# Up-projections of a latent attention group: plain float32 products against three float32r products of split operands

## The reference, cut to what matters

```
proj = h @ w_in                                   # all projections of both groups
q_a, ckv, krope, g_a, q_b, k_b, v_b, ... = split(proj)
ckv = rmsnorm(ckv, kv_gain)                       # 512 latent columns per row
q_lat = einsum('bthn,hnc->bthc', q_a[..., :128], w_uk)
s = einsum('bthc,bsc->bhts', q_lat, ckv) + einsum('bthr,bsr->bhts', q_rope, krope)
p = softmax(where(chunk_mask, s * 192 ** -0.5, -inf))
o_lat = einsum('bhts,bsc->bthc', p, ckv)
o_a = einsum('bthc,hvc->bthv', o_lat, w_uv)       # 8 heads of 128
```

## Time and profile before

| | |
|---|---|
| time, median of 3 runs | 908.91 us |
| span of the profiled execution | 907.6 us |
| PE busy | 883.5 us, 97% |
| DVE busy | 414.4 us, 46% |
| ACT busy | 322.4 us, 36% |
| DMA read from HBM, written | 175.93 MB, 12.69 MB |
| share of L1926 (`kn`) and L1935 (`vm`) in the chain that ended last | 2% each |

### The profile page before, as it was taken

How to read it: one execution, slowest core, us unless ns; L and a number is a source line. 1 busy time by engine, 2 the same in 40 slices (tenths; PEclk the granted TensorE clock), 3 DMA queues, 4 the chain that set the end, 5 groups by cost and what they waited for, 6 DMA issues and landing times.

```text
span 907.6 us, 13732 instructions
## 1 busy us (share of the span) xinstructions
PE 883.5 (97%) x5564; PEld 769.2 (85%) x5564; DVE 414.4 (46%) x851; ACT 322.4 (36%) x599; POOL 117.3 (13%) x187
## 2 busy tenths in 40 slices
PE   4999999999999999999999999999999999999996
PEld 1567688999998688888999989999999998888886
DVE  3523343336322145443333368364455566677362
ACT  3232352434321234222322264232334345554252
POOL 0000012101100000112120401000122223530000
PEclk9999999999999999999999999999999999999998
DMA  9999957464443122557552476655798833793313
GB/s 362 409 409 408 409 204 248 155 244 157 143 139 105 69 75 88 175 161 238 167 168 91 123 285 235 243 186 186 257 305 283 269 133 111 282 295 124 135 59 127
DMA packets 53439, 187.43 MB, mean 207 GB/s; under 512 B 7776, under 2 KB 8408, under 8 KB 52224
## 3 DMA queue, kind: packets, MB, share of 16 engines
q1 hardware_dynamic: 39456, 141.35, 43.0%
q0 software_dynamic: 13776, 44.68, 15.3%
q10 hardware_dynamic: 144, 0.52, 0.1%
HBM read 175.93 MB, written 12.69 MB: 208 GB/s over the span
## 4 chain that ended last, share of the span: by engine, by line
PE 89%; DMA 5%; DVE 3%; ACT 2%; issue 1%; SPq 0%; ACTq 0%; DVEq 0%
PE proj L1824 34%; PE proj L1813 29%; DMA araw<-in_units 5%; PE bankO L1794 3%; PE proj L1845 2%; PE proj L1794 2%; PE bankO L1926 2%; PE bankO L1935 2%; PE bankS L1845 1%; PE bankS L1989 1%; PE bankS L1824 1%; PE bankO L2008 1%; PE bankO L2016 1%; PE bankO L2007 1%; PE bankO L1976 1%
## 5 line engine op out<-in xcount | busy, mean ns | idle before, releaser
L1305 DVE TENSOR_TENSOR w_lo<-raw,w_hi 128x1024 fp32r<-128x1024 f32 (+2 forms) x164 | 196.9, 1205 | 236.7 <-ACT w_hi L986 235.9
L986 ACT ACTIVATE w_hi<-raw 128x1024 fp32r<-128x1024 f32 (+2 forms) x164 | 167.8, 1026 | 196.9 <-PE proj L1813 99.3
L1824 PE MATMUL proj<-hT_hi,w_hi 128*128 128x384 f32 x608 | 211.0, 347 | 0.0
L1824 PE MATMUL proj<-hT_hi,w_lo 128*128 128x384 f32 x608 | 203.8, 335 | 0.0
L1824 PE MATMUL proj<-hT_lo,w_hi 128*128 128x384 f32 x608 | 203.4, 335 | 0.0
L1813 PE MATMUL proj<-w_hi,hT_hi 128*128 128x512 f32 (+2 forms) x464 | 177.9, 384 | 0.5 <-DVE hT_lo L1564 0.4
L1813 PE MATMUL proj<-w_hi,hT_lo 128*128 128x512 f32 (+2 forms) x464 | 173.6, 374 | 0.0
L1813 PE MATMUL proj<-w_lo,hT_hi 128*128 128x512 f32 (+2 forms) x464 | 173.4, 374 | 0.0
L1824 PEld LDWEIGHTS proj<-hT_hi,w_hi 128*128 128x128 f32 x608 | 114.2, 188 | 9.5 <-issue 7.8
L1824 PEld LDWEIGHTS proj<-hT_lo,w_hi 128*128 128x128 f32 x608 | 114.3, 188 | 0.5 <-issue 0.2
L1824 PEld LDWEIGHTS proj<-hT_hi,w_lo 128*128 128x128 f32 x608 | 114.1, 188 | 0.0
(11 more groups left out here) (363 smaller groups left out, 1050.8 us busy)
## 6 DMA issues: line engine op xcount, KB each, us to landing
raw<-in_units SPq DMA_DIRECT2D x184, 512.0 KB, 4.1
araw<-in_units SPq DMA_DIRECT2D x64, 512.0 KB, 10.6
kcT<-in_dsa_k_t POOLq DMA_DIRECT2D x8, 512.0 KB, 6.4
vc<-in_cache_dsa_v POOLq DMA_DIRECT2D x8, 512.0 KB, 5.7
gate_scratch<-stage POOLq DMA_DIRECT2D x8, 384.0 KB, 3.8
raw<-in_units SPq DMA_DIRECT2D x8, 336.0 KB, 3.9
raw<-in_units SPq DMA_DIRECT2D x8, 320.0 KB, 4.9
x_sb<-in_x_prompt SPq DMA_DIRECT2D x2, 1024.0 KB, 6.1
```

The costliest lines, as they stand in the source:

```text
L986: return nc.scalar.activation(out, in_, func, scale=scale, **kw)
L1305: V.tensor_tensor(w_lo[:, SLOT[u], 0:w], raw_of(u)[:, 0:w], high(u)[:, 0:w].bitcast(F32), ALU.subtract).then_inc(lo_ready, 1)
L1824: ins = mm(banks[blk][:, 0:TOK], w[:, n, cols], a[:, kt, :], start=first and n == m == 0, stop=final and n == per - 1 and m == 2)
```

## The change

Every operand of the prompt's up-projections gets a high and a low half in float32r, and each plain float32 matmul becomes three float32r matmuls.

- `ckT` 0 and 1: ACT copies the bank as `ckv_hi`, DVE subtracts it from the bank for `ckv_lo`. The sample rows (`ckT` 2) stay plain.
- New step `uks` h, on the unit of `kn` h: ACT makes `wuk_hi` (128 x 512) of the head's `wukT`, DVE writes `wuk_lo` over `wukT`. `kn` h on PE now waits for DVE's half.
- New step `uvs` 0 to 3, on units 99, 101, 103 and 111: the same for a quarter of `wuvT` (128 x 1024 each). `wuv_lo` overwrites `wuvT`.
- Since `wuvT` is overwritten, POOL loads it a second time after `vm` for `oa` (four DMAs of 512 KB); `ld_krc`, which waits for the last `mp`, moves behind these. The first loading is listed earlier (units 87, 89, 91, 93).

```diff
@@ plan()
     for n in range(CB):
-        put(u + 15 + 4 * n, ("ld_uvT", n))
+        put(u + 13 + 2 * n, ("ld_uvT", n))
...
         if h:
-            put(u + h, ("kn", h - 1))
+            put(u + h, ("uks", h - 1), ("kn", h - 1))
+    for n, v in enumerate((LAST_UNIT["m1", 0] - 4, LAST_UNIT["m1", 0] - 2, LAST_UNIT["m1", 0], u + 2)):
+        put(v, ("uvs", n))
...
-    put(u, ("ld_krc", 0))
+    for n in range(CB):
+        put(u + 1 + n, ("ld_uvT", CB + n))
+    put(u + HEADS, ("ld_krc", 0))
@@ buffers
-    ckvT = at("ckvT", 37, [P, CB, TOK])
+    ckv_hi, ckvT = at("ckv_hi", 37, [P, CB, SEQ], F32R), at("ckvT", 41, [P, CB, P])
+    ckv_lo = at("ckv_lo", 70, [P, CB, SEQ], F32R)
+    wuv_hi = [at(f"wuv_hi{q}", kib, [P, HEADS * HD], F32R) for q, kib in enumerate((82, 86, 90, 62))]
+    wuv_lo = at("wuv_lo", 0, [P, CB, HEADS * HD], F32R)
+    wuk_hi = [at(f"wuk_hi{n}", kib, [P, CB, HD], F32R) for n, kib in enumerate((74, 95.5))]
+    wuk_lo = at("wuk_lo", 66, [P, 2, CB, HD], F32R)
@@ POOL
         def ld_uvT(q):
-            pool.wait_ge(unit_used, LAST_UNIT["ada", 3] + 1)
-            load(wuvT[:, q, :], i["w_uv_t"][:, q, :], "wuvT_in")
+            if q < CB:
+                pool.wait_ge(unit_used, LAST_UNIT["ada", 3] + 1)
+            else:
+                filled(pool, "vm", 3)
+            load(wuvT[:, q % CB, :], i["w_uv_t"][:, q % CB, :], "wuvT_in")
@@ ACT
         def ckT(t):
             filled(act, "ckT", t, "T")
+            if t < 2:
+                copy(ckv_hi[:, :, P * t:P * (t + 1)], turned).then_inc(sem("ckv_hi_ready"), 1)
+            else:
+                copy(ckvT[:], turned).then_inc(free["T"], 1)
+        def uks(h_):
+            act.wait_ge(sem(f"wukT_in{h_ % 2}"), 16 * (h_ // 2 + 1))
+            if h_ >= 2:
+                filled(act, "kn", h_ - 2)
+            copy(wuk_hi[h_ % 2][:], wukT[:, h_ % 2]).then_inc(sem("wuk_hi_ready"), 1)
+        def uvs(q):
+            if q == 0:
+                act.wait_ge(sem("wuvT_in"), 16 * CB)
+                act.wait_ge(sem("ckvn_ready"), NT)
...
+            copy(wuv_hi[q][:], wuvT[:, q, :]).then_inc(sem("wuv_hi_ready"), 1)
@@ DVE
+        def uks(h_):
+            dve.wait_ge(sem("wuk_hi_ready"), h_ + 1)
+            V.tensor_tensor(wuk_lo[:, h_ % 2], wukT[:, h_ % 2], wuk_hi[h_ % 2][:].bitcast(F32),
+                            ALU.subtract).then_inc(sem("wuk_split"), 1)
+        def uvs(q):
+            dve.wait_ge(sem("wuv_hi_ready"), q + 1)
+            V.tensor_tensor(wuv_lo[:, q, :], wuvT[:, q, :], wuv_hi[q][:].bitcast(F32),
+                            ALU.subtract).then_inc(sem("wuv_split"), 1)
@@ PE
         def kn(h_):
-            pe.wait_ge(sem(f"wukT_in{h_ % 2}"), 16 * (h_ // 2 + 1))
+            pe.wait_ge(sem("wuk_split"), h_ + 1)
...
             for q in range(CB):
-                ins = mm(out[:, 0:SEQ], wukT[:, h_ % 2, q, :], ckvT[:, q, 0:SEQ], start=q == 0, stop=q == CB - 1)
+                for m, (w, a) in enumerate(((hi_, ckv_hi), (hi_, ckv_lo), (lo_, ckv_hi))):
+                    ins = mm(out[:, 0:SEQ], w[:, q, :], a[:, q, :], start=q == m == 0, stop=q == CB - 1 and m == 2)
         def vm_(n):
...
-                pe.wait_ge(sem("wuvT_in"), 16 * CB)
+                pe.wait_ge(sem("wuv_split"), CB)
...
+                for m, (a, w) in enumerate(((ckv_hi, hi_), (ckv_hi, lo_), (ckv_lo, hi_))):
+                    ins = mm(out[:], a[:, q, rows], w, start=q == m == 0, stop=q == CB - 1 and m == 2)
```

More of the change, by code:

```diff
@@ L1081, in ckT @@
             filled(act, "ckT", t, "T")
-            copy(ckvT[:, :, P * t:P * (t + 1)],
-                 bank["T"][:].rearrange("p (k q) -> p k q", q=P)).then_inc(free["T"], 1)
+            turned = bank["T"][:].rearrange("p (k q) -> p k q", q=P)
+            if t < 2:
[11 more added lines that the diff above has]
+                act.wait_ge(sem("ckvn_ready"), NT)
+            if q == 2:
+                act.wait_ge(sem("bias_out"), 16)
+            if q == 3:
+                filled(act, "qrsT", 0)
+            copy(wuv_hi[q][:], wuvT[:, q, :]).then_inc(sem("wuv_hi_ready"), 1)
         def kiT_(t):
@@ L1220, in kl @@
                  bank["T"][:].rearrange("p (h s) -> p h s", s=P)).then_inc(free["T"], 1)
-        steps = {"bias": bias, "xsq": xsq, "xr": xr, "h": h, "ckn": ckn, "ckT": ckT,
+        steps = {"bias": bias, "xsq": xsq, "xr": xr, "h": h, "ckn": ckn, "ckT": ckT, "uks": uks, "uvs": uvs,
                  "kiT": kiT_,
@@ L1388, in ckn, with ckT @@
                                        in1=kvg[:], op0=ALU.mult, op1=ALU.mult).then_inc(sem("ckvn_ready"), 1)
+        def ckT(t):
+            if t < 2:
+                dve.wait_ge(sem("ckv_hi_ready"), t + 1)
+                rows = slice(P * t, P * (t + 1))
+                V.tensor_tensor(ckv_lo[:, :, rows], bank["T"][:].rearrange("p (k q) -> p k q", q=P),
+                                ckv_hi[:, :, rows].bitcast(F32), ALU.subtract).then_inc(free["T"], 1)
+        def uks(h_):
[6 more added lines that the diff above has]
+                            ALU.subtract).then_inc(sem("wuv_split"), 1)
         def rotate(out, src, cos, sin, w):
@@ L1496, in st @@
             V.tensor_copy(ckvcT[:, b % 3, :, P:NKEY],
-                          ckvT[:, :, SEQ + DS * b:SEQ + DS * (b + 1)]).then_inc(sem("st_new"), 1)
+                          ckvT[:, :, DS * b:DS * (b + 1)]).then_inc(sem("st_new"), 1)
         def sample_max(kind, b):
@@ L1655, in dsn @@
             V.tensor_tensor(out, out, bank["O"][:].rearrange("p (h q) -> p h q", q=P), ALU.add).then_inc(free["O"], 1)
-        steps = {"h": h, "hl": hl, "dsn": dsn, "xsq": xsq, "xr": xr, "rb": rb, "xT": xT, "xS": xS, "modT": modT_, "ckn": ckn, "rk": rk, "rq": rq,
+        steps = {"h": h, "hl": hl, "dsn": dsn, "xsq": xsq, "xr": xr, "rb": rb, "xT": xT, "xS": xS, "modT": modT_, "ckn": ckn, "ckT": ckT, "uks": uks, "uvs": uvs, "rk": rk, "rq": rq,
                  "kn": kn, "mp": mp, "dp": dp, "mv": mv, "dv": dv, "ql": ql, "krc": krc_, "st": st, "ss": ss, "ds": ds,
@@ L1919, in kn @@
         def kn(h_):
-            pe.wait_ge(sem(f"wukT_in{h_ % 2}"), 16 * (h_ // 2 + 1))
+            pe.wait_ge(sem("wuk_split"), h_ + 1)
             if h_ == 0:
                 pe.wait_ge(sem("ckv_out"), 32)
+                emptied(pe, "ckT", 1)
             out = take("kn", h_, "O")
+            hi_, lo_ = wuk_hi[h_ % 2], wuk_lo[:, h_ % 2]
             for q in range(CB):
-                ins = mm(out[:, 0:SEQ], wukT[:, h_ % 2, q, :], ckvT[:, q, 0:SEQ], start=q == 0, stop=q == CB - 1)
+                for m, (w, a) in enumerate(((hi_, ckv_hi), (hi_, ckv_lo), (lo_, ckv_hi))):
+                    ins = mm(out[:, 0:SEQ], w[:, q, :], a[:, q, :], start=q == m == 0, stop=q == CB - 1 and m == 2)
             ins.then_inc(full["O"], 1)
@@ L1932, in vm_ @@
             if n == 0:
-                pe.wait_ge(sem("wuvT_in"), 16 * CB)
+                pe.wait_ge(sem("wuv_split"), CB)
+            rows, cols = slice(P * t, P * (t + 1)), slice(512 * g, 512 * (g + 1))
             for q in range(CB):
-                ins = mm(out[:], ckvT[:, q, P * t:P * (t + 1)], wuvT[:, q, 512 * g:512 * (g + 1)], start=q == 0,
-                         stop=q == CB - 1)
+                hi_, lo_ = wuv_hi[q][:, cols], wuv_lo[:, q, cols]
+                for m, (a, w) in enumerate(((ckv_hi, hi_), (ckv_hi, lo_), (ckv_lo, hi_))):
+                    ins = mm(out[:], a[:, q, rows], w, start=q == m == 0, stop=q == CB - 1 and m == 2)
             ins.then_inc(full["O"], 1)
@@ L2011, in oa @@
         def oa(n):
+            if n == 0:
+                pe.wait_ge(sem("wuvT_in"), 2 * 16 * CB)
             out = take("oa", n, "O")
```

## The result

Sixteen runs of the changed kernel have a median of 911.7 us (910.18 to 913.33), sixteen runs of the kernel before 909.23 us (908.87 to 909.76). The ratio is 1.0027, with an interval from 1.0021 to 1.0034: slower by 2.5 us, a small loss but clear of the scatter, where 0.8 us were forecast. The 16 runs don't scatter evenly. Two took 910.18 and 910.28 us, eleven 911.20 to 911.96, three 913.02 to 913.33: three steps, 1.4 and 1.6 us apart by their means, with nothing between them. The mean granted clock of TensorE (PE) in each run points the same way, though it is coarse: 0.997 in the two lowest runs, 0.996 or 0.997 in the eleven, 0.994 or 0.995 in the three highest. The recorded execution took 911.89 us with a span of 910.0, so it is one of the middle step.

A forecast was written before the change was run, and what follows sets the result against it. PE, busy for 97% of the span, was taken as the bound. Terms -2.4 - 2.8 + 5.0 + 1.0 = +0.8 us on 908.9 gave 909.7 us, with an 8-in-10 range from 907.0 to 911.5.

The forecast's parts named there:

- the two stops: Units 111 and 115: PE waits 2.50 us ahead of `kn` 1 and `kn` 5, as ACT's copy follows an eviction; 5.0 us.
- the clock falls in the stop: Rival: after each 2.5 us stop, the next unit's products take another 4.17 us, twice; 918.0 us, chance 0.04.
- The third of the prediction's own signs of being wrong: The prediction counts itself wrong if the granted clock falls between 220 and 320 us.
- That rival's sentence on the Trainium skill: An idle engine is set back to half its clock; the clock rival comes true if 2.5 us were idle enough.
- Float32 pace removed, -5.2 us: PE's `kn` and `vm`: float32r matmuls at 0.119 and 0.228 us save 2.4 and 2.8 us.
- The other size for it: Gain on `kn` and `vm` by the skill's isolated matmul gaps, 109 and 216 ns: 6.7 us, sum 1.5 us better.
- The float32 rows for 512 columns: Copy and subtraction taken as 633 and 692 ns; with 640-column float32r rows, a stop would be 2.73 us.
- `rk`, +1.0: Units 103 to 105: `uvs` 2 delays DVE's split and `rk`, so PE stands still for 1.0 us; bounds 0.8 and 1.3.
- Unit 112, slack 0.5: Behind the stop, `uvs` 3 also on DVE: halves ready 0.5 us before PE wants `kn` 2; no cost.
- ACT, DVE, POOL and DMA elsewhere, nothing: Ordinary units' halves are ready first; the second `wuvT` load, unit loads and `ld_krc` cost nothing.
- 1.3 us around the span: The runs' median was taken as 1.3 us above the profiled span.

The follow-up runs named there:

- stops of 2.1 us: Kernel before, with DVE making three additions of 384 columns into scratch ahead of each of the eight `kn`, which wait for them: 934.27 us, ratio 1.0272.
- 0 of 8 at 1.5 us: Kernel before, with DVE making two additions of 384 columns into scratch ahead of each of the eight `kn`, which wait for them: 921.46 us, ratio 1.0135.
- 8 of 8 at 3.9 us: Kernel before, with DVE making six additions of 384 columns into scratch ahead of each of the eight `kn`, which wait for them: 957.40 us, ratio 1.0531.
- The filled stops: Changed kernel with nine unused float32 matmuls of `ones` (128 columns) on PE ahead of the waits of `kn` 1 and `kn` 5: 910.06 us, ratio 1.0009.
- the kernel without stops: Changed kernel with every `uks` one unit earlier and `uvs` 2 moved from unit 103 to 109: 904.04 us, ratio 0.9944.
- the kernel with one stop: Changed kernel with only the half for `kn` 5 one unit earlier, leaving the stop at unit 111: 908.94 us, ratio 0.9993.
- eight stops of 2.7 us: Kernel before, with DVE making four additions of 384 columns into scratch ahead of each of the eight `kn`, which wait for them: 942.39 us, ratio 1.0370.

## Why the prediction was wrong

**The step that failed** is the cost of the two stops. The sum counts their length alone, 2 x 2.50 us, and puts the clock at nothing; it stands only as the rival "the clock falls in the stop", which was wrong in its chance and in its price. It was set at 0.04, with the argument that a stop of 2.5 us is shorter than the 3 us that the clock held behind PE's last matmul. That row shows one stop only. The third of the prediction's own signs of being wrong came true: the granted clock fell between 220 and 320 us, at 254.0. Seventeen of 32 stops in the 16 runs drew a fall (read from the steps), and with stops of 2.1 us 5 of 8. One sample at one length was read as a bound, while the share of stops with a fall grew here from 0 of 8 at 1.5 us to 8 of 8 at 3.9 us. So not the rival but the forecast should have carried it: about one fall in two stops, 1.6 us, which makes 911.3, near the 911.7 measured. The price was mis-sized too. The whole of the next unit's products at half pace would be 4.17 us, twice 8.3; the recorded low stretches behind stops of up to 2.7 us all ended after 3.4 us, so a fall costs 1.6 us, and two falls make 909.7 + 3.2 = 912.9 us, not 918.0. The error in the chance made the forecast too low, the error in the price would have made it too high.

That rival's sentence on the Trainium skill, "TensorE: Matmul & The Clock Gate", section "Part 1: The HAM clock gate", had the direction right, though the rule as told there gives no chance for a stop of 2.5 us. The page calls the lower clock the default of an array that isn't busy, and activity what lifts it. The filled stops agree: `kn` as late as before, array busy, no fall in 11 runs.

The prediction also says that only the end of the trace of before bears on this rival. The start bears on it too. PE's first matmul there comes behind a wait of 13.3 us, and the first matmuls are slow:

```profile
16.95 1.06 PE L1873 MATMUL bankT<-eye,x_sb 128*128 128x128 f32 x4
...
18.96 0.66 PE L1873 MATMUL bankS<-eye,x_sb 128*128 128x128 f32 x4
```

Four records of one form take 1.06 us and, two microseconds later, 0.66. The windows read a granted clock of 1.00 there from the first microsecond on, so they don't say whether it was the clock. A wait that long says nothing of one of 2.5 us either, but it was a warning that work behind a wait can run slow.

The other steps, against what the trace shows:

- *Float32 pace removed, -5.2 us*: right. 0.119 and 0.226 us a matmul, and 5.3 us gained once nothing stands in the way. The other size for it, 6.7 us by the isolated matmul gaps, is refuted by the same rows.
- *Stops at units 111 and 115, 2.50 us each*: right. 2.47 us; `wuk_hi` begins 0.75 us behind the eviction's start and lasts 0.63, `wuk_lo` 0.69. The float32 rows for 512 columns were the right choice over the 640-column ones.
- *`rk`, +1.0*: right. DVE's `wuv_lo` and the split follow at 214.50 and 215.65, `rk` begins at 217.00 (predicted 216.97), and the transposes effectively at 221.22 (221.26), as their second one starts at 221.33 and the two were 0.11 us apart in before. Moving `uvs` 2 gave 905.37 - 904.04 = 1.3 us, a little more.
- *Unit 112, slack 0.5*: right. `wuk_lo` for `kn` 2 is done at 257.54, and without the fall PE would have wanted it at 252.60 + 5.60 = 258.20, less 0.18 for the hand-over: 0.48 us.
- *ACT, DVE, POOL and DMA elsewhere, nothing*: right, by the kernel without stops.
- *1.3 us around the span*: off. The recorded execution of after has 911.89 - 910.0 = 1.9 us, and runs of the kernel before with spans of 907.3 to 907.4 us took 909.1 to 909.2. So the distance is 1.8 us, and the execution recorded before, with its span of 907.6, was one of some 909.4 us. For the sum, which adds a difference to the median, this matters by nothing. But the median of three runs, 908.91 us, lay 0.3 us below that of sixteen, and the forecast with it.

Taken together the sum gives 909.2 + 0.8 = 910.0 us without a fall, where the two lowest runs are 910.18 and 910.28, and 911.6 us with one, where the median is 911.7. Of the 2.0 us between the forecast and the median, 1.6 are the fall and 0.3 the median of three runs.

## What to carry to other kernels

When a change makes a dense PE stand still, weigh a price for the clock beside the length of the stop. Here it was nothing for stops that cost 1.5 us, and for those of 2.5 us a fall of 1.6 us in about half of them. A profile of before that shows no such stop says nothing against it. Before that, look in the list of the engine that prepares the operand: one place earlier, ahead of an eviction that waits for PE itself, the same copy costs nothing, and the change goes from 2.5 us lost to 5.3 us gained. Run times that lie on equal steps are a sign that the same event does or doesn't happen, and its price is the height of a step.

## What was unexpected

- Stops that cost 1.5 us drew no fall in 8, those of 2.1 us 5 in 8, those of 2.7 us 7 in 8, those of 3.9 us 8 in 8; in the changed kernel, at 2.5 us, about half did. The order is clear. The shares rest on one trace each, and the run times agree with them: with two additions all four runs lie within 0.3 us, with three additions three of them within 0.4 us and one, 932.54 us, about a fall lower.
- The fall shows up to 1.4 us after PE is at work again (252.60 to 254.0), so the slow rows stand under innocent instructions and no wait row names them. The longer durations and wider starts in the timeline do, and the granted clock by windows.
- Each low stretch lasted 3.4 us, at the longest stops in turn 6.8 and 3.4. What decides, at equal length of a stop, whether the clock falls was not settled; neither were the two runs of the kernel with one stop, and the one with eight stops of 2.7 us, that lie off the steps.
